# The last weight sum of a pair of steps: written by VectorE into its own buffer in three feed-forward stages

## The reference

```python
def swiglu(x, w_gu, w_down):
    gate, up = jnp.split(x @ w_gu, 2, axis=-1)
    return (jax.nn.silu(gate) * up) @ w_down
...
x = x + 0.5 * swiglu(rms_norm(x, ffn1_norm[l]), ffn1_w_gu[l], ffn1_w_down[l])
```

## Time and profile before

| | us |
|---|---|
| median of 3 runs (lowest, highest) | 1271.41 (1269.85, 1274.66) |
| the profiled execution's own time | 1271.68 |
| its span in the trace | 1269.9 |
| PE busy | 1258.7 (99%) |
| VectorE (DVE) busy | 993.1 (78%) |
| ScalarE (ACT) busy | 840.6 (66%) |
| GpSimd (POOL) busy | 68.6 (5%) |

### The profile page before, as it was taken

One profiled execution on the slowest core, in us unless ns is written; L12 is line 12 of the kernel. 1 busy time (PEld: TensorE's weight loads), 2 busy tenths in 40 slices (PEclk: granted clock), 3 DMA queues, 4 the chain that ended last, 5 costly groups with the idle time before them and its releaser, 6 DMA issues.

```text
span 1269.9 us, 17171 instructions
## 1 busy us (share of the span) xinstructions
PE 1258.7 (99%) x6858; PEld 1050.9 (83%) x6858; DVE 993.1 (78%) x1151; ACT 840.6 (66%) x1083; POOL 68.6 (5%) x100
## 2 busy tenths in 40 slices
PE   9999999999999999999999999999999999999998
PEld 7888888889988888887788887888888898888887
DVE  5888777877657988786488878679887798688885
ACT  7576658766556666686466667666666857766763
POOL 0000000000000000000000011000000100000000
PEclk9999999999999999999999999999999999999999
DMA  9987748887786798868688777768899989867772
GB/s 345 321 317 224 253 161 277 282 257 231 186 304 242 257 299 295 307 221 269 232 287 309 232 255 198 271 255 248 302 305 300 321 245 273 312 207 263 270 248 73
DMA packets 49278, 331.89 MB, mean 261 GB/s; under 512 B 5484, under 2 KB 7788, under 8 KB 10160
## 3 DMA queue, kind: packets, MB, share of 16 engines
q1 hardware_dynamic: 34512, 230.88, 47.6%
q0 software_dynamic: 13536, 97.27, 31.0%
q10 hardware_dynamic: 1152, 2.66, 0.6%
HBM read 329.73 MB, written 65.02 MB: 311 GB/s over the span
## 4 chain that ended last, share of the span: by engine, by line
PE 83%; DVE 5%; issue 5%; DMA 5%; ACT 1%; POOL 0%; SPq 0%; DVEq 0%; POOLq 0%; ACTq 0%
PE ps L2924 21%; PE ps L2926 21%; PE ps L2925 21%; PE ps L2834 8%; DMA arena<-in_tiles 5%; DVE w_lo_part L1759 3%; PE ps L3057 2%; PE ps L2850 1%; PE ps L2953 1%; PE ps L2945 1%; PE ps L2958 1%; PE ps L568 1%; PE ps L570 1%; PE ps L569 1%; ACT w_hi_part L700 1%
## 5 line engine op out<-in xcount | busy, mean ns | idle before, releaser
L1759 DVE TENSOR_TENSOR w_lo_part<-w_raw,w_hi_part 128x2048 fp32r<-128x2048 f32 (+2 forms) x181 | 409.1, 2265 | 49.0 <-ACT w_hi_part L700 48.8
L700 ACT ACTIVATE w_hi_part<-w_raw 128x2048 fp32r<-128x2048 f32 (+1 forms) x180 | 340.8, 1897 | 85.1 <-PE ps L2926 70.5
L2924 PE MATMUL ps<-w_hi_part,x_hi 128*128 128x512 f32 (+1 forms) x680 | 267.7, 394 | 1.3 <-ACT mem_kv L1263 0.8
L2926 PE MATMUL ps<-w_hi_part,x_lo 128*128 128x512 f32 (+1 forms) x680 | 258.8, 381 | 0.0
L2925 PE MATMUL ps<-w_lo_part,x_hi 128*128 128x512 f32 (+1 forms) x680 | 258.2, 380 | 0.0
L700 ACT ACTIVATE w_hi_part<-arena 128x2048 fp32r<-128x2048 f32 x78 | 148.3, 1914 | 84.2 <-DMA arena<-in_tiles 52.2
L1759 DVE TENSOR_TENSOR w_lo_part<-arena,w_hi_part 128x2048 fp32r<-128x2048 f32 x78 | 177.4, 2288 | 27.1 <-ACT w_hi_part L700 26.7
L2924 PE MATMUL ps<-w_hi_part,h_hi_part 128*128 128x512 f32 x464 | 183.9, 396 | 0.0
L2926 PE MATMUL ps<-w_hi_part,h_lo_part 128*128 128x512 f32 x464 | 180.9, 390 | 0.0
L2925 PE MATMUL ps<-w_lo_part,h_hi_part 128*128 128x512 f32 x464 | 180.7, 389 | 0.0
L2926 PEld LDWEIGHTS ps<-w_hi_part,x_lo 128*128 128x128 f32 x680 | 127.8, 188 | 25.1
(11 more groups left out here) (457 smaller groups left out, 1602.6 us busy)
## 6 DMA issues: line engine op xcount, KB each, us to landing
w_raw<-in_tiles SPq DMA_DIRECT2D x176, 1024.0 KB, 6.7
made_sums<-in_tiles POOLq DMA_DIRECT2D x60, 1024.0 KB, 8.3
arena<-made_sums SPq DMA_DIRECT2D x30, 1024.0 KB, 7.1
arena<-in_tiles POOLq DMA_DIRECT2D x21, 1024.0 KB, 10.4
arena<-in_tiles SPq DMA_DIRECT2D x9, 1024.0 KB, 8.5
mem_kv<-in_tiles POOLq DMA_DIRECT2D x6, 1024.0 KB, 11.0
w_raw<-in_tiles SPq DMA_DIRECT2D x3, 512.0 KB, 5.9
arena<-in_w_ukv POOLq DMA_DIRECT2D x1, 1536.0 KB, 6.7
```

The lines of the kernel that those rows point to most:

```text
L700: nc.scalar.activation(WH[:, n % RING, 0:w], source(n), ACT.Copy).then_inc(S["w_hi"], 1)
L1759: nc.vector.tensor_tensor(WL[:, n % RING, 0:w], source(n), WH[:, n % RING, 0:w], ALU.subtract).then_inc(S["w_split"], 1)
L2924: nc.tensor.matmul(o, a_hi, w_hi, start=start, stop=False, skip_group_check=True)
L2926: return nc.tensor.matmul(o, a_lo, w_hi, start=False, stop=stop, skip_group_check=True)
```

## The change

In ffn1, ffn3 and ffn4 the accumulating DMA is gone. VectorE makes T4 into a buffer of its own (PB[3]) by a `tensor_tensor` add, `t4`; ScalarE's `w_hi` of m4 waits for that. The raw buffer of m2's tile is now given back only when `t4` has read it. VectorE's list is changed in two places: in the first pair `t4` stands between the low parts of m1 and p3; at each of the three borders it stands behind `t2`, the low part of m4 comes ahead of `c22`, and the two `hidden` products come ahead of the low part of m2. ffn2 keeps the DMA and its VectorE order. In all four stages the tile of p3 is loaded ahead of those of m2 and m1 from the second pair on, into the buffer that has been held longest.

```diff
+    for name in QUADS:
+        for s in steps_of(name)[1:]:
+            early = next(k for k, (n, _) in enumerate(ring) if n == unit_of[name, "p3", s])
+            first = next(k for k, (n, _) in enumerate(ring) if n == unit_of[name, "m2", s])
+            ring.insert(first, ring.pop(early))
...
+                if kind == "m4" and name != "ffn2":
+                    return PB[3]
...
-                if r >= RING:
-                    old = ring[r - RING][0]
+                old = raw_old[n]
+                if old is not None:
                     sp.wait_ge(S["w_split"], old + 1)
...
+                    if old in kind_of and kind_of[old][0] in QUADS and kind_of[old][0] != "ffn2" and kind_of[old][1] == "m2":
+                        sp.wait_ge(S["sums"], sum_no[kind_of[old][0], "t4", kind_of[old][2]])
...
-                        if n == unit_of[name, "p3", s]:
+                        if n == unit_of[name, "m1", s]:
                             sp.wait_ge(S["w_split"], unit_of[name, "m7", s - 2] + 1)
                             t_load(name, s, 1)
...
+                def t4(s):
+                    n = at("m2", s)
+                    dve.wait_ge(S["sums"], sum_no[name, "t2", s])
+                    dve.wait_ge(w_loaded[raw_slot[n]], 16 * raw_load[n])
+                    nc.vector.tensor_tensor(PB[3], ta_of(name, s), RAW[:, raw_slot[n], :], ALU.add).then_inc(S["sums"], 1)
+
+                def border(s):
+
+                    if name == "ffn2":
+                        c22(s)
+                        w_lo(at("m4", s))
+                        w_lo(at("p5", s + 2))
+                        t2(s + 2)
+                        w_lo(at("m2", s + 2))
+                    else:
+                        w_lo(at("m4", s))
+                        c22(s)
+                        w_lo(at("p5", s + 2))
+                        t2(s + 2)
+                        t4(s + 2)
+                    hidden(s, 1, bank(4)[:, CW:], SG[:, 1, :])
+                    hidden(s + 1, 1, P5F[:, CW:], P5F[:, 0:CW])
+                    if name != "ffn2":
+                        w_lo(at("m2", s + 2))
...
                     t2(3)
                     w_lo(at("m1", 3))
+                    t4(3)
                     w_lo(at("p3", 3))
...
-            t4_sum("ffn3", 3)
             split("ffn3", "m4", 3)
             add("ffn3", 7)
```

More of the change, by code:

```diff
@@ L106, in quad_sums @@
 def quad_sums(name):
-    return [("s", 0), ("s_lo", 0)] + [(which, s) for s in steps_of(name) for which in ("t2", "c11", "c12", "c22")]
+    return [("s", 0), ("s_lo", 0)] + [(which, s) for s in steps_of(name) for which in ("t2", *(() if name == "ffn2" else ("t4",)), "c11", "c12", "c22")]
 def paired_order():
@@ L251, in program @@
         ends[name] = n_tiles
-    ring_no = {n: r for r, (n, _) in enumerate(ring)}
+    for name in QUADS:
[3 more added lines that the diff above has]
+            ring.insert(first, ring.pop(early))
+    raw_slot, raw_load, raw_old = {}, {}, {}
+    held, loads = [None] * RING, [0] * RING
+    for n, _ in ring:
+        k = min(range(RING), key=lambda j: -1 if held[j] is None else held[j])
+        loads[k] += 1
+        raw_slot[n], raw_load[n], raw_old[n] = k, loads[k], held[k]
+        held[k] = n
     gu_no = {(name, s): k for k, (name, kind, s) in enumerate(key for key in unit_of if key[1] == "g1")}
@@ L537, in t4_added @@
         def t4_added(name, s):
-            return S["t_added"], 16 * (2 * n_pairs + quad_no(name, s) + 1)
+            return S["t_added"], 16 * (2 * n_pairs + steps_of(name).index(s) + 1)
         def t1_at(name):
@@ L557, in source @@
         def source(n):
-            if n in ring_no:
-                return RAW[:, ring_no[n] % RING, 0:width(n)]
+            if n in raw_slot:
+                return RAW[:, raw_slot[n], 0:width(n)]
             return pair_source(*kind_of[n])
@@ L629, in _ @@
                         sp.wait_ge(S["sums"], sum_no[kind_of[old][0], "t2", kind_of[old][2]])
+                    if old in kind_of and kind_of[old][0] in QUADS and kind_of[old][0] != "ffn2" and kind_of[old][1] == "m2":
+                        sp.wait_ge(S["sums"], sum_no[kind_of[old][0], "t4", kind_of[old][2]])
                 w = width(n)
-                sp.dma_start(RAW[:, r % RING, 0:w], d["tiles"][t, :, 0:w]).then_inc(w_loaded[r % RING], 16)
+                sp.dma_start(RAW[:, raw_slot[n], 0:w], d["tiles"][t, :, 0:w]).then_inc(w_loaded[raw_slot[n]], 16)
                 if n == unit_of["ffn2", "g1", 4]:
@@ L691, in w_hi @@
                     return
-                if n in ring_no:
-                    act.wait_ge(w_loaded[ring_no[n] % RING], 16 * (ring_no[n] // RING + 1))
+                if n in raw_slot:
+                    act.wait_ge(w_loaded[raw_slot[n]], 16 * raw_load[n])
                 else:
@@ L702, in pair_ready @@
             def pair_ready(name, kind, s):
-                if name in QUADS and kind == "m6":
-                    act.wait_ge(S["sums"], sum_no[name, "t2", s])
+                if name in QUADS and (kind == "m6" or kind == "m4" and name != "ffn2"):
+                    act.wait_ge(S["sums"], sum_no[name, {"m6": "t2", "m4": "t4"}[kind], s])
                 elif name in QUADS:
@@ L1981, in t2 @@
                 def t2(s):
-                    r = ring_no[at("p3", s)]
+                    n = at("p3", s)
                     dve.wait_ge(S["w_split"], at("p5", s) + 1)
-                    dve.wait_ge(w_loaded[r % RING], 16 * (r // RING + 1))
+                    dve.wait_ge(w_loaded[raw_slot[n]], 16 * raw_load[n])
                     a = pair_source(name, "m6", s)
-                    nc.vector.tensor_tensor(a, a, RAW[:, r % RING, :], ALU.add).then_inc(S["sums"], 1)
+                    nc.vector.tensor_tensor(a, a, RAW[:, raw_slot[n], :], ALU.add).then_inc(S["sums"], 1)
+                def t4(s):
+                    n = at("m2", s)
+                    dve.wait_ge(S["sums"], sum_no[name, "t2", s])
+                    dve.wait_ge(w_loaded[raw_slot[n]], 16 * raw_load[n])
+                    nc.vector.tensor_tensor(PB[3], ta_of(name, s), RAW[:, raw_slot[n], :], ALU.add).then_inc(S["sums"], 1)
[16 more added lines that the diff above has]
+                        w_lo(at("m2", s + 2))
                 def c11(s):
@@ L2049, in from_three @@
                     w_lo(at("d", 2))
[L2050 to L2056, removed]
+                    border(3)
                     w_lo(at("m1", 5))
@@ L2068, in from_three @@
                     hidden(6, 0, C12F[:, CW:], C12F[:, 0:CW])
-                    c22(5)
                 def from_five():
@@ L2122, in from_five @@
                     w_lo(at("d", 4))
-                    c22(5)
                 from_five() if name == "ffn2" else from_three()
[L2126 to L2131, removed]
+                border(5)
                 w_lo(at("m1", 7))
@@ L2143, in quad_ffn @@
                 hidden(8, 0, C12F[:, CW:], C12F[:, 0:CW])
[L2144 to L2150, removed]
+                border(7)
                 w_lo(at("m1", 9))
@@ L4193, in _ @@
             make("ffn2", 2)
-            t4_sum("ffn1", 3)
             split("ffn1", "m4", 3)
             copy("ffn2", 3)
-            t4_sum("ffn1", 5)
             split("ffn1", "m4", 5)
             add("ffn2", 3)
-            t4_sum("ffn1", 7)
             split("ffn1", "m4", 7)
             copy("ffn2", 4)
-            t4_sum("ffn1", 9)
             pool.wait_ge(S["tile_used"], unit_of["ffn1", "m7", 9] + 1)
@@ L4230, in _ @@
             copy("ffn3", 7)
-            t4_sum("ffn3", 3)
             split("ffn3", "m4", 3)
             add("ffn3", 7)
-            t4_sum("ffn3", 5)
             split("ffn3", "m4", 5)
             copy("ffn4", 0)
-            t4_sum("ffn3", 7)
             split("ffn3", "m4", 7)
             add("ffn4", 0)
-            t4_sum("ffn3", 9)
             make("ffn4", 1)
@@ L4253, in _ @@
             make("ffn4", 7)
-            for s in steps_of("ffn4"):
-                t4_sum("ffn4", s)
 def layout(a):
```

## The result

| | before | changed |
|---|---|---|
| median (lowest to highest), 4 runs each | 1272.36 (1269.85 to 1274.66) | 1289.38 (1288.87 to 1289.9) |
| ratio of the medians | | 1.013, 95% interval 1.0115 to 1.0145 |
| span of the profiled execution | 1269.9 | 1287.3 |

A forecast was written before the change was run, and what follows sets the result against it. TensorE, busy 99% of the span, was taken as the bound. First pairs 8.7 us plus borders 9.5 less removed waits 2.2 gave +16.0 on 1271.68, stated as 1287.5 us, range 1279 to 1295.

The forecast's parts named there:

- rule on the DRAIN: Twelve sums on VectorE: no start before the pipeline is empty, 0.08 us more each, 1.0 in all, result 1288.7 us.
- p3.3: First pair of ffn1, ffn3, ffn4: product starts late behind its low part, delayed by t4; 1.41 us lost.
- m6.3: First pair, next product: TensorE waits for c11, which follows the delayed low parts; 0.1 us.
- d.1: First pair, down tile: its load is held until t4 has read the raw buffer; product 1.37 us late.
- rival (b): Held load of the first pair lands late, 6.9 us instead of 4.8: 6.3 us more, 1293.8 us; chance 0.10.
- Nine borders: Borders within ffn1, ffn3, ffn4: m2's low part ends late behind VectorE's gapless row; 1.06 us each, 9.5 in all.
- Removed waits: TensorE's transposes no longer wait for hidden behind the accumulating DMAs; 2.2 us gained.
- d.7 in ffn3: Last pair: load beside earlier made sums and bias copy could be 0 to 3 us late, once; taken as 0.
- 9.7: Loads of ffn3's last pair beside made sums and bias copy: said to take 6.9 to 9.7 us in company.
- 6.15 us: Held load of the first pair by the documented bandwidth: 1.35 us more in each stage, an estimate of 1291.6 us.
- Rival (c): Not slower: t4 fits into VectorE's idle time, only the 2.2 us of waits go, 1269.5 us; chance 0.05.

The follow-up runs named there:

- late_t4: Changed kernel with first-pair t2 and t4 earlier, later pairs' t4 behind the first down tile's low part; 1273.25 us, ratio to before 1.0008; timed again 1273.84 us, 1.0009.
- t4_before_m1: Changed kernel with the first pair's t4 one place earlier, ahead of the low part of m1.3; 1288.41 us, ratio to the kernel before 1.0131.
- border_old_order: Changed kernel with VectorE's order of before at the borders, t4 put in behind t2; 1297.26 us, ratio to the kernel before 1.019.
- paced form: late_t4 with ffn4's made sums held back on GpSimd's queue until m6 of ffn3's last pair is split; 1272.03 us, ratio to before 1.0.

## Why the prediction was right

The working was right in its mechanism, and each of its terms can be laid beside a wait. One slip stands in its sum: 1271.68 + 16.0 is 1287.7 and not 1287.5; the 1288.7 by the rule on the DRAIN starts from 1287.7.

- **p3.3, 1.41 forecast.** 1.51 in all three stages. VectorE did what was worked out (low part moved by 2.20); the 0.10 more is the hand-over: 0.15 us from the end of the low part to the product, not the 0.05 that I took from a VectorE row. At all other late products it is 0.05. p3.3 alone among them has a wait for a snapshot in front of it as well; that this makes the difference is argued, not tried.
- **m6.3, 0.1 forecast.** No wait. TensorE wants `c11` for it, which ended at 870.85 + 0.68 = 871.53, and it started at 871.72. p3.3 had itself come 0.10 later than forecast and ran 0.12 longer, so the 0.1 was covered.
- **d.1, 1.37.** 1.25, 1.27 and 1.20. The load landed in 4.8 us in each; rival (b), a late landing, falls for this place.
- **Nine borders, 1.06.** 1.03 each, 9.3 us against 9.5.
- **Removed waits, -2.2.** In the trace of before, m2.7 and m2.9 of the three stages wait in sum 2.23 us beyond the 0.36 that a row of transposes always takes; none of this is left. It is also what the first profile of late_t4 showed in its three stages (2.1).
- **Not in the sum.** d.7 in ffn3, 1.38, which stood in the range as "0 to 3 us late, once" and was taken as 0. Here (b)'s mechanism did appear: ring loads in company of the made sums took up to 16.2 us, more than the 9.7 that I had as a bound. And the first matmuls after a wait run slower: p3.3 takes 2.84 us instead of 2.72, d.1 and d.7 5.57 instead of 5.44, 0.9 us in all at these seven places.

The waits after: 4.5 + 3.7 + 9.3 + 1.4 = 18.9, plus 0.9, less 2.2, is 17.6 us; the three stages grew by 17.7. Nothing of size is left open.

The rule on the DRAIN (the Trainium skill, "VectorE: DVE Perf Modes") would have had the next instruction start no sooner than the end of the one before. The rows after show starts of 864.25, 866.45 and 868.65 beside lengths of 2.28: 2.20 apart again. That was half of what the section says: the same paragraph adds that "A next op that is not held starts earlier", and with this the rows agree. The total of 1288.7 lies nearer to the measured one, but by other causes. The 6.15 us that the Trainium skill, "DMA: Bandwidth & Descriptors", gives among its measured bandwidths for 1 MB issued from GpSimd was not seen on the held load, which SyncE issues and which took 4.8.

Rival (c), `t4` in idle time, failed for the places that the change chose, by the slack that was forecast (0.84 against 2.20); late_t4 shows that the same sum in the same stages costs nothing that can be measured where the spare time is (ratios 1.0 to 1.0009 in three measurements).

## What to carry to other kernels

In this kernel an engine that is busy 83% of a stage had room for more work only at the places where its results are early; measure the distance from each result to its use, and put the new instruction ahead of a result that has more to spare than the instruction takes. Moving a sum from a DMA to an engine also keeps its source buffer longer: follow the next load into that buffer to its first use. And a queue that gets free early starts its next transfers early, beside loads that had had less company.

## What was not expected of the hardware

**The clock fell after some waits of 2 us.** In t4_before_m1 TensorE waited for 2.06 us ahead of m1.3 in each of three stages. In ffn3 the granted clock then read as follows (stretch, length, busy PE, PEld, DVE, ACT, POOL, clock, DMA):

```profile
866.00:870.00 4.00, 2.23 (x10) 1.50 (x8) 4.00 (x3) 3.16 (x2) 0.00 (x0) 1.00 0.22 35
870.00:873.00 3.00, 2.87 (x8) 2.25 (x9) 3.00 (x3) 1.21 (x3) 0.00 (x0) 0.59 1.04 429
873.00:876.00 3.00, 3.00 (x13) 2.41 (x12) 2.16 (x2) 1.16 (x1) 0.00 (x0) 0.84 1.02 371
876.00:879.00 3.00, 3.00 (x15) 2.49 (x14) 2.21 (x1) 2.17 (x2) 0.00 (x0) 1.00 0.48 202
```

The first matmul of m1.3 behind the wait, and two neighbouring ones in that stretch:

```profile
870.13 0.50 PE L2946 MATMUL ps<-w_hi_part,x_hi 128*128 128x512 f32 x1 [1.90 <-DVE w_lo_part L1774]
...
871.25 0.63 PE L2946 MATMUL ps<-w_hi_part,x_hi 128*128 128x512 f32 x1
871.68 0.63 PE L2947 MATMUL ps<-w_lo_part,x_hi 128*128 128x512 f32 x1
```

They start 0.43 us apart instead of 0.227, so the engine ran at its lower level, 1.2 GHz, for some 3 us, and m1.3 took 4.44 us instead of 2.84. The same wait in ffn1 and ffn4 was not followed by a fall, nor were the waits of 1.5 us in the changed kernel.

The same execution has a second fall, in ffn0, which the change doesn't touch: TensorE waited 2.0 us behind a sum that landed late, and from 71.8 on its matmuls too start 0.43 us apart:

```profile
72.00:74.00 2.00, 2.00 (x6) 1.52 (x6) 2.00 (x2) 1.49 (x1) 0.00 (x0) 0.50 0.45 188
74.00:76.00 2.00, 2.00 (x8) 1.57 (x7) 2.00 (x2) 0.00 (x0) 0.54 (x1) 0.69 0.05 8
```

The like wait in ffn0 of border_old_order and of late_t4, 2.3 us each, was not followed by a fall. So of these six waits of 2.0 to 2.3 us ahead of a product two were: a wait of 2 us can cost 1.6 us more than itself, but need not. What decides it is open.

**Landing times differ between executions.** Of three profiles of late_t4 and its paced form, one had a late sum by DMA in ffn0 and two a late tile at the start of ffn4, each worth 1 to 3 us of TensorE's time. The late sum in ffn0 stands in 3 of the 12 traces of all kernels. A single profile can't tell a gain of 2 us in this kernel.
